# A hybrid recurrent layer on one Trainium2 core: the S5 part on 64-row quadrants with moves by transfers, and the first two input chunks from the unnormalized input

## Time and profile before

| | us |
|---|---|
| median of 3 runs | 351.1 |
| the three runs | 351.09, 353.65, 351.1 |
| the profiled execution | 353.67 |
| its span in the trace | 351.8 |
| TensorE busy | 330.3 |
| VectorE busy | 236.1 |
| ScalarE busy | 121.0 |

### The profile page before, as it was taken

The page is one execution under the profiler, slowest core; times in us unless marked ns, Lnnn a source line. Parts: engine busy times, 40 slices in busy tenths (PEclk is TensorE's granted clock), DMA queues, the critical chain, the costliest instruction groups (busy, mean ns, idle before and its releaser), DMA issues.

```text
span 351.8 us, 6392 instructions
## 1 busy us (share of the span) xinstructions
PE 330.3 (94%) x2546; PEld 280.9 (80%) x2546; DVE 236.1 (67%) x501; ACT 121.0 (34%) x262; POOL 43.4 (12%) x81
## 2 busy tenths in 40 slices
PE   7899998889999999989979999999999999989991
PEld 6688876667889898869967888887888989877990
DVE  2574499986628978485749727596644897686454
ACT  4243001150691003583412620115177010566321
POOL 4018530006000000250000000000600000120000
PEclk9999999999999999899999999999999999999997
DMA  8977622232531500799915472322262242476503
GB/s 281 380 258 229 241 95 86 61 109 72 163 111 61 180 2 2 240 199 273 351 39 159 141 268 91 119 80 102 92 182 64 102 136 66 124 192 120 184 1 123
DMA packets 28013, 50.85 MB, mean 145 GB/s; under 512 B 6288, under 2 KB 6864, under 8 KB 27984
## 3 DMA queue, kind: packets, MB, share of 16 engines
q1 hardware_dynamic: 25968, 44.06, 37.9%
q0 software_dynamic: 1728, 6.29, 7.5%
q10 hardware_dynamic: 288, 0.09, 0.1%
HBM read 46.80 MB, written 3.64 MB: 143 GB/s over the span
## 4 chain that ended last, share of the span: by engine, by line
PE 75%; DVE 13%; POOL 4%; ACT 4%; issue 2%; DMA 1%; DVEq 0%; POOLq 0%; ACTq 0%
PE pr L490 41%; PE pr L764 10%; DVE att L1327 2%; PE wk L557 2%; DVE h L1059 2%; PE wk L679 2%; PE wk L504 2%; PE wk L725 2%; POOL lev L1577 2%; PE wk L602 1%; POOL lev L1579 1%; PE wk L570 1%; DMA x<-in_xt 1%; PE wk L671 1%; PE wk L617 1%
## 5 line engine op out<-in xcount | busy, mean ns | idle before, releaser
L490 PE MATMUL pr<-h,wring 128*128 128x264 f32 x768 | 178.9, 389 | 3.2 <-DVE h L1059 3.2
L490 PEld LDWEIGHTS pr<-h,wring 128*128 128x128 f32 x768 | 143.3, 190 | 30.0 <-issue 5.9
L764 PE MATMUL pr<-a_hi,w_hi 128*128 128x264 f32 x96 | 27.6, 288 | 0.0
L764 PE MATMUL pr<-a_lo,w_hi 128*128 128x264 f32 x96 | 27.2, 283 | 0.0
L764 PE MATMUL pr<-a_hi,w_lo 128*128 128x264 f32 x96 | 27.2, 283 | 0.0
L877 ACT ACTIVATE v<-pr 128x264 f32<-128x264 f32 x12 | 4.7, 388 | 48.2 <-PE pr L490 48.2
L865 ACT ACTIVATE h<-x 128x264 f32<-128x264 f32 x24 | 9.5, 420 | 32.8 <-DVE x L1480 30.7
L948 ACT ACTIVATE zs<-pr 128x264 f32<-128x264 f32 x16 | 6.0, 384 | 41.7 <-PE pr L490 41.7
L1327 DVE COPY_PREDICATED att<-masks,wk 128x512 f32<-128x512 int32 x20 | 17.6, 950 | 1.0
L764 PEld LDWEIGHTS pr<-a_lo,w_hi 128*128 128x128 f32 x96 | 18.1, 188 | 0.1
L764 PEld LDWEIGHTS pr<-a_hi,w_hi 128*128 128x128 f32 x96 | 18.1, 188 | 0.1
(11 more groups left out here) (281 smaller groups left out, 539.6 us busy)
## 6 DMA issues: line engine op xcount, KB each, us to landing
wring<-in_w_in SPq DMA_DIRECT2D x100, 256.0 KB, 3.0
wring<-in_w_out SPq DMA_DIRECT2D x20, 256.0 KB, 3.7
w_hi<-in_w_out POOLq DMA_DIRECT2D x6, 512.0 KB, 4.3
w_lo<-in_w_out POOLq DMA_DIRECT2D x6, 512.0 KB, 7.8
x<-in_xt SPq DMA_DIRECT2D x2, 528.0 KB, 4.7
out_y<-h SPq DMA_DIRECT2D x4, 264.0 KB, 2.0
s5m_t<-in_s5m SPq DMA_DIRECT2D x2, 512.0 KB, 4.4
ss<-in_hg_in SPq DMA_DIRECT2D x2, 512.0 KB, 4.0
```

Of the source, the lines that this page charges most:

```text
L490: mm = nc.tensor.matmul(ring_bank(layer, i)[:, 0:TT], wring[:, slot, n, :], act_in[:, k, :], start=(k == 0), stop=(k == KT - 1))
L764: mm = nc.tensor.matmul(ring_bank(layer, i)[:, 0:TT], w[:, j % WSLOTS, n, :], a[:, k, :], start=(k == 0 and p == 0), stop=(k == KT - 1 and ...
```

## The change

Four things, in one program.

1. **Chunks 0 and 1 from x times the weights.** `xw` (over `zs`) holds x times `norm_w` without the factor per token. VectorE makes it, in layer 0 ScalarE the upper four tiles, in layer 1 VectorE right after each residual. TensorE starts chunk 0 from it and puts the mean's two products into the middle: after the sixth product in layer 0, after the fourth in layer 1 (`SUM_AT`). Chunk 1 uses `xw` too. The factor per token is multiplied in when VectorE, no longer ScalarE, brings the two chunks out (`first_chunks`), behind `scale_x`. In layer 0 the squares are now added on VectorE as in the others, and `s5_steps` waits for the parameters alone.
2. **S5 per group, without zeros.** A group of 16 channels and 64 states takes 64 rows: `s5m_t` is 128 x 4 x 8 x 16, `ca`, `bb`, `gtr` and `tmat` are half as wide. Every product becomes two of 64x64 (or 64x16), one on rows and columns 0 to 63, one on 64 to 127, into the same bank.
3. **Moves by transfers.** `u` is written by ScalarE in the order of the tokens within a block (four small operations a chunk, straight from PSUM), goes out to memory in one transfer, and comes back into `ub` by eight. The response goes into `tmat` by eight transfers. GELU's result goes out by ten transfers and comes back by one, with tokens still sorted by their place in the block, which `s5_mix` undoes. All of these are on SyncE. `s5_relay` and both `s5_back` are gone; the factor 0.5 moved into the gate.
4. **Loads.** The S5 matrices come by eight transfers of 16-column pieces, in layer 0 after chunk 5 instead of chunk 1, for layer 1 after the sixth output chunk.

```diff
+            def project_first(layer):
+                ring_free(pe, layer, C_F0)
                 for k in range(KT):
...
+                    scaled_by_weight(pe, layer, k)
+                    mm = nc.tensor.matmul(ring_bank(layer, C_F0)[:, 0:TT], wring[:, slot, n, :], xw[:, k, :],
+                                          start=(k == 0), stop=(k == KT - 1))
...
+                    if k == SUM_AT[layer]:
+                        mean_square(layer)
@@ s5_turn, s5_response, s5_inputs
-                for r in range(4):
-                    for n in range(4):
-                        src = (bb_re, bb_im)[r // 2][:, 4 * (r % 2) + n, :, :]
-                        mm = nc.tensor.transpose(wk[:, r, P * n:P * n + P], src.rearrange("p j c -> p (j c)"), c("ident"))
+                for n, src in enumerate((bb_re, bb_im)):
+                    for s in range(S5T):
+                        for g in range(2):
+                            rows = slice(64 * g, 64 * g + 64)
+                            mm = nc.tensor.matmul(wk[rows, n, 64 * s:64 * s + 64], src[rows, s, :, :].rearrange("p j c -> p (j c)"),
+                                                  c("ident")[rows, rows], start=True, stop=True)
...
+                            mm = nc.tensor.matmul(wk[64 * g:64 * g + GC, 4, 64 * s:64 * s + 64], b[rows, s, 0, :],
+                                                  ca[rows, s, 0:SL, :].rearrange("p j c -> p (j c)"),
+                                                  start=(n == 0), stop=(n == 1), skip_group_check=True)
...
-                pe.wait_ge(u_ready, layer + 1)
-                pe.wait_ge(gtr_evac, layer * 4 + 4)
+                pe.wait_ge(u_in, 16 * 8 * (layer + 1))
+                pe.wait_ge(gtr_evac, layer * 2 + 2)
...
-                        mm = nc.tensor.matmul(wk[:, 2 * n + s // 4, a:a + NS + SC], gtr[:, n, s, :], ub[:, s, 0:NS + SC],
-                                              start=True, stop=True)
+                        for g in range(2):
+                            rows = slice(64 * g, 64 * g + 64)
+                            mm = nc.tensor.matmul(wk[rows, 2 * n + s // 4, a:a + NS + SC], gtr[rows, n, s, :], ub[rows, s, 0:NS + SC],
+                                                  start=True, stop=True)
@@ s5_outputs
+                    for k, (w, data) in enumerate(parts):
+                        for g in range(2):
+                            rows = slice(64 * g, 64 * g + 64)
+                            mm = nc.tensor.matmul(wk[rows, 4, a:a + 72], w[rows], data[rows], start=(k == 0), stop=(k == 2),
+                                                  skip_group_check=True)
@@ glu_gate
-                pe.wait_ge(yg_ready, layer + 1)
-                pe.wait_ge(yg_act, layer + 1)
+                pe.wait_ge(yg_in, 16 * (layer + 1))
@@ SyncE
+            def s5_matrices(layer):
+                for g in range(2):
+                    rows = slice(64 * g, 64 * g + 64)
+                    for i in range(4):
+                        sp.dma_start(s5m_t[rows, i, :, :], s5m[layer, rows, i, :, GC * g:GC * g + GC]).then_inc(s5m_in, 16)
+            def u_to_rows(layer):
+                chunk_out(sp, layer, C_U1)
+                sp.dma_start(u_rows[layer].rearrange("(t p) x -> p t x", p=P), u[:, :, :]).then_inc(u_out, 16)
...
+                sp.wait_ge(u_out, 16 * (layer + 1))
+                for g in range(2):
+                    rows = u_rows[layer].rearrange("(s g c) x -> g c s x", g=2, c=GC)[g]
+                    for q, (src, to) in enumerate(((slice(192, 264), slice(0, NS + SC)), (slice(64, 128), slice(NS, NS + SC)),
+                                                   (slice(0, 64), slice(NS, NS + SC)), (slice(128, 200), slice(NS, NS + SC + NS)))):
+                        at = 64 * g + GC * q
+                        sp.dma_start(ub[at:at + GC, :, to], rows[:, :, src]).then_inc(u_in, 16)
+            def block_kernel(layer):
+                sp.wait_ge(resp_ready, layer + 1)
+                for g in range(2):
+                    for q in range(SL):
+                        at = 64 * g + GC * q
+                        sp.dma_start(tmat[at:at + GC, :, GC * (3 - q):], resp[64 * g:64 * g + GC, :, 0:GC * (q + 1)]).then_inc(tmat_in, 16)
+            def y_from_rows(layer):
+                sp.wait_ge(yb_ready, layer + 1)
+                yv = yb.rearrange("p (s k) -> p s k", s=S5T)
+                for g in range(2):
+                    rows = y_rows[layer].rearrange("(s g c) x -> g c s x", g=2, c=GC)[g]
+                    for j in range(SL):
+                        at = 64 * g + GC * j
+                        sp.dma_start(rows[:, :, SC * j:SC * j + SC], yv[at:at + GC, :, 0:SC]).then_inc(y_out_rows, 16)
+                    sp.dma_start(rows[:, :, TP:TT], yv[64 * g:64 * g + GC, :, SC:]).then_inc(y_out_rows, 16)
+                sp.wait_ge(y_out_rows, 16 * 10 * (layer + 1))
+                sp.dma_start(yg[:, :, :], y_rows[layer].rearrange("(t p) x -> p t x", p=P)).then_inc(yg_in, 16)
...
                     chunk(w_in[layer, i])
+                    if i == NCH - 3:
+                        u_to_rows(layer)
+                    if i == NCH - 1:
+                        block_kernel(layer)
...
-                    if i == 3 and layer + 1 < DEPTH:
+                    if i == 3:
+                        y_from_rows(layer)
+                    if i == 5 and layer + 1 < DEPTH:
                         sp.wait_ge(glu_done, layer + 1)
-                        sp.dma_start(s5m_t[:, :, :, :], s5m[layer + 1]).then_inc(s5m_in, 16)
+                        s5_matrices(layer + 1)
@@ VectorE
+            def scale_by_weight(layer, k):
...
+                step(ts(xw[:, k, :], x[:, k, :], par(Q_NORM + layer * KT + k), None, ALU.mult), xw_ready)
+            def first_chunks(layer):
+                for i, dst in ((C_F0, x3[:, 0, :]), (C_LR, lr_t)):
+                    dve.wait_ge(proj_done, layer * NCH + i + 1)
+                    step(tt(dst, ring_bank(layer, i)[:, 0:TT], rstd, ALU.mult), first_evac)
@@ VectorE, s5_within
-                for q in range(4):
-                    for half in range(2):
-                        src = wk[32 * half:32 * half + 32, 4, :].rearrange("p (s m) -> p s m", s=4)[:, :, 0:32 * (q + 1)]
-                        step(cp(qrt(tmat, q)[:, 4 * half:4 * half + 4, 32 * (3 - q):P], src))
-                settle()
-                for s in range(S5T):
-                    step(stt(out=tmat[:, s, :], in0=c("rev"), scalar=par(Q_S5D + layer * S5T + s), in1=tmat[:, s, :],
-                             op0=ALU.mult, op1=ALU.add), tmat_ready if s == S5T - 1 else None)
...
+                for g in range(2):
+                    rows = slice(64 * g, 64 * g + GC)
+                    step(tt(resp[rows, :, 0:GC], resp[rows, :, 0:GC], skip[rows], ALU.add), resp_ready if g else None)
@@ VectorE, the start
             dve.wait_ge(par_in, 16)
+            s5_steps()
+            for k in range(KH):
+                scale_by_weight(0, k)
+            for m in range(1, KT - 1):
+                sum_squares(0, m)
             dve.wait_ge(cst_in[0], 16)
-            s5_steps()
             for layer in range(DEPTH):
                 scale_x(layer, Q_NORM + layer * KT, h_ready)
+                first_chunks(layer)
```

More of the change, by code:

```diff
@@ L518, in project_low_rank @@
                         mm = nc.tensor.matmul(ring_bank(layer, C_LR)[32 * n:32 * n + 32, 0:TT], wring[:, slot, n, 0:32],
-                                              h[:, KH * half + n, :], start=(half == 0), stop=(half == 1))
+                                              xw[:, KH * half + n, :], start=(half == 0), stop=(half == 1))
                     mm.then_inc(proj_done if half else half_done, 1)
             def low_rank(layer):
-                pe.wait_ge(chunk_evac, layer * NCH + C_LR + 1)
+                chunk_out(pe, layer, C_LR)
                 if layer == 0:
@@ L868, in norm @@
                             high_part(n - 1, j)
+                if n == 0:
+                    act.wait_ge(par_in, 16)
+                    for k in range(KH, KT):
+                        step(fn(xw[:, k, :], x[:, k, :], ACT.Copy, scale=par(Q_NORM + k)), xw_act)
                 act.wait_ge(ms_done, n + 1)
@@ L938, in turned, with s5_turned @@
                         wk[:, 4, 0:n].rearrange("p (a b c) -> p a b c", a=dst.shape[1], b=dst.shape[2]), ACT.Copy), tr_evac)
[L940 to L944 removed]
+            def s5_turned(layer):
+                for n in range(2):
+                    act.wait_ge(gtr_done, layer * 2 + n + 1)
+                    step(fn(gtr[:, n, :, :].rearrange("p s m -> p (s m)"), wk[:, n, :], ACT.Copy), gtr_evac)
             def silu(layer, i):
@@ L1036, in _ @@
                         sines(sinc, cosc)
-                        s5_turned(layer, range(4))
+                        s5_turned(layer)
                 use_logs()
@@ L1451, in head_gates @@
             def head_gates(layer, tiles):
```

(10 more changed lines are left out.)

209 lines of the change are left out of this document (106 added, 103 removed).

## The result

The changed kernel takes **360.2 us** (median of 4 runs, 359.05 to 361.91). In the same runs the kernel before took 351.1 (4 runs, 350.23 to 353.65). The ratio is 1.024, with a 95% interval of 1.019 to 1.030: slower, and above the forecast range (346 to 358.5). The profiled execution took 361.91, with a span of 359.9.

A forecast was written before the change was run, and what follows sets the result against it. Besides TensorE's products, GpSimd's sines before 46 us, the entry of layer 1 and each layer's end bound the kernel. Terms of -0.5, -2.2, -2.7, +1.4 and +1.7 sum to -2.3: 353.67 becomes 351.4 us, range 346 to 358.5.

The forecast's parts named there:

- the S5 output: End of each layer: y's trip takes 10.0 us, TensorE stands 3.0, gate product starts 0.7 later; +1.4 in all.
- still in time: On SyncE, the sample values queued behind the new S5 transfers would still arrive in time; no cost given.
- Rival C: Both legs of y's trip at 4.2 make 13.4 us, gate product 4.1 late per layer: 358.2 us, chance 0.15.
- The clock: Gate product after TensorE's stand: granted clock falls to 0.50 in both layers, new in layer 1; +1.7 us.
- The front: Entry of layer 0: early products lost to sines ending at 44.1, regained by lighter VectorE; -0.5 us.
- The waits of the later levels: Layer 0, before the turned keys: TensorE's 3.8 us of waits go because VectorE's work is 5.6 us less.
- The entry of layer 1: From the last residual: chunk 0 starts at once with the mean in its middle; -2.2 us, bounds -1.5 and -2.5.
- The products: Compact S5 products ahead of the scan: 30 ns a quadrant instruction, -1.35 us a layer, -2.7 in all.
- Rival B: S5 quadrants of a pair do not overlap, 54 to 61 ns an instruction: 365.9 us, chance 0.15.
- The input moves: S5 input path by transfers takes about 10 us, hidden behind about 16 us of products; costed at nothing.

The follow-up runs named there:

- Experiment 2: The changed kernel with GpSimd's loads of split weights held until y is back: 359.7 us, ratio 1.019 to the kernel before.
- kernel 10: The changed kernel with S5 phases ahead of the first scaling, five of y's ten writes issued by ScalarE, and the gate product behind chunk 24: 342.6 us, ratio 0.972.
- experiment 4: The changed kernel with fifteen filler products of 264 columns where TensorE stands ahead of the gate product: 356.9 us, ratio 1.011 to the kernel before.
- Experiment 7: The changed kernel with VectorE's S5 phases ahead of the first scaling in layer 0, TensorE averaging all squares: 355.2 us, ratio 1.007 to the kernel before.
- experiment 1: The changed kernel without the S5 output's ten writes and read back, its S5 output left out of the result: 344.3 us, ratio 0.975 to the kernel before.
- kernels 3: The changed kernel with five of y's ten writes issued by ScalarE's queue and five by SyncE's: 355.6 us, ratio 1.011 to the kernel before.
- 9: The changed kernel with the gate product and ScalarE's tanh moved behind projection chunk 24: 352.0 us, ratio 1.000 to the kernel before.
- kernel 12: The changed kernel with S5 phases ahead of the first scaling and the gate product behind chunk 24, all ten writes on SyncE: 348.8 us, ratio 0.986.
- kernel 11: The kernel before (old S5 part) with chunks 0 and 1 from x times the weights, early S5 phases and the gate product behind chunk 24: 351.2 us, ratio 0.995.

## Why the prediction was wrong

**The step that failed** is the S5 output: the landing of the last write first, and how far GELU's end lies ahead of TensorE second. The forecast took 1.9 us for the landing, from a 64 KB state store, with "GpSimd's weight loads on the same engines" counted only in the read back. It measured 5.74 and 6.55. With the issues (4.2 instead of 5.0) and the read back (2.70 and 2.85 instead of 3.0) the trip became 12.7 and 13.7 us instead of 10.0. Experiment 2 shows the cause in layer 0, where the write lands in 1.56 once the loads are held; in layer 1 it accounts for 3 us of 6.55.

That is 2.7 and 3.7 of the 4.2 and 4.6 us by which TensorE stood longer than forecast. The other 1.5 and 0.9 lie ahead of the trip. The forecast had GELU end 7.0 us ahead of TensorE's arrival at the gate product, and it was 5.5 and 6.1. In the kernel before VectorE starts on the sample values (L1378) with no wait; now it waits for them:

```profile
DVE qm L1467 <- DMA qm<-sample_values: 2.3, 2, 1.5
```

The two waits are 1.48 us in layer 0 and 0.86 in layer 1, just the difference. On SyncE the sample values are issued behind the eight pieces of the response, in layer 0 from 115.74 instead of 113.08. The forecast had them "still in time". That their lateness made GELU late is read from the chain; no run moves them. In kernel 10 VectorE waits for them as long (2.2 us in all), but y is back in time all the same.

Two readings of the kernel before would have shown the landing. First, the view of transfers that gave has two more small stores of states, and their medians are no 1.9:

```profile
out_hgp<-s SPq DMA_DIRECT2D x2, 64.0 KB, 7.1
...
out_glap<-s SPq DMA_DIRECT2D x2, 32.0 KB, 7.8
```

In layer 0 they are issued at 150.05 and 150.74, behind GpSimd's first load of the low parts (148.53) and two weight loads of SyncE's, and land in 11.4 and 11.1 us. Second, GpSimd's timeline shows when the loads of the high parts begin, and what releases them (L691, the last retention output):

```profile
140.24 1.88 POOL L1633 DMA_DIRECT2D w_hi<-in_w_out  x3 [52.92 <-PE wk L691]
```

The forecast's last write goes out at 133.8 + 5.0 = 138.8, ahead of that. But in the same sum TensorE is 2.3 us earlier, and the loads follow TensorE: they begin at 137.9, and the last write is behind them. Measured were 136.45 and 137.85. The forecast moved the write and left the loads where they were.

Rival C came nearest, with a trip of 13.4 us and +4.1 a layer, at a chance of 0.15. It had the length, but from both legs at 4.2; one was longer than that and the other shorter.

**The clock** was right in kind, for both layers, and small in size. The forecast had 1.7 for the gate product and the means of layer 1 and nothing for layer 0, where the clock was low before too; measured were 2.5 and 0.8 (the table). The Trainium skill (TensorE: Matmul & The Clock Gate, the section on the HAM clock gate) has the fall as the default that activity lifts; the trace agrees, with 0.50 at the end of the stand in layer 0, 0.57 over the stretch of layer 1, and 1.00 in experiment 4.

**The front.** The total of layer 0 was right (-0.4 at the turned keys against -0.5), with errors that cancel. The sines ended at 42.0, not 44.1: GpSimd began them 2.9 us later than before and was 1.3 faster through them. The waits of the later levels went, as forecast, but the first grew to 4.7 us, more than the three of 3.9 in all. It lasts from 43.1 to 47.85, and the granted clock is 0.60 from 44 to 52:

```profile
47.85 1.12 PE L695 MATMUL wk<-qe,k 64*128 64x64 f32 x8 [4.74 <-DVE qe L1405]
```

It ends 5.9 us behind the sines, as before; TensorE only came to it earlier. Experiment 7 takes it away with early sines. The entry of layer 1 was right: -2.5, the bound named, against -2.2.

**The products** were right in all: 30 to 34 ns a quadrant against 30, and 7.1 us less up to the gate products against 7.3. Rival B, at 54 to 61 ns, is out. The Trainium skill (TensorEngine Tiling (Array Packing), Gotcha 1) would have had different row tiles kept out of one PSUM bank; here two quadrants that differ in rows and columns write one bank at 31 ns each, so they overlap. No run tried two row tiles with the same columns.

**The input moves** did not stop TensorE, as said: the inputs start at 109.32 with no wait ahead of them. They were not free, though. The pieces of the response are what the sample values stand behind on SyncE: in layer 1 the chain runs through them (the eight of L464 take 5.7 us to issue, from 275.10) to the sample values, VectorE's sample states and GELU, which is the 1.5 and 0.9 us above.

**Not tested.** No run has the quadrants without the transfers, so what each is worth alone is open; experiment 1 comes nearest, with 9 us for all but the output's trip.

## What to carry to other kernels

A copy replaced by a transfer must be priced as issue, landing and read back, each at the time of day at which it runs, and by all rows of its kind: here the forecast took a store that landed in 1.9 us and passed over two with medians of 7.1 and 7.8. When a change makes the bounding engine reach a point earlier, move everything that this engine releases as well: in the changed kernel the last 4 KB went out 1.4 us behind the first of 1.5 MB of loads, in kernel 10 1.5 us ahead of them. Ask also what stands behind new transfers on the queue that issues them. And a remedy is tried on the old layout too: the early phases help with both S5 parts, the late gate only where y is late.

## What the runs showed of the hardware

- In the kernel after, the writes of y (32 KB, and two of 4 KB a layer) landed in 1.5 to 1.8 us as long as they were issued ahead of GpSimd's three loads of 512 KB, and in 4.2 to 6.6 behind the first of these. With the loads held the last one took 1.56 us in layer 0 and 3.60 in layer 1; in kernel 10, 1.1 us ahead of the loads of layer 1, it took 4.0. What delayed these last two is open.
- A read of 264 KB took 2.7 to 3.0 us behind the loads or with the loads held, and 4.1 to 9.3 with loads of GpSimd beside it (kernels 3, 9, 10 and 12).
- Two 64x64 quadrants on different rows and columns, in one PSUM bank, ran at 30 to 34 ns an instruction.
- While TensorE stood for 7 us the clock fell to 0.50. One stand of 1.2 us behind products of two and four columns was enough in layer 1 of kernel 11 and layer 0 of kernel 10 (2.13 us for the four products behind it), and not in the other layer of each, nor in kernel 12 (1.16 us). Fifteen filler products kept it at 1.00.
- In the kernel after, SyncE's issues took 0.34 to 0.44 us each for the writes of y, and 0.60 to 0.69 for the pieces of the response, but once 1.08 and once 1.70.
